# Row sums on VectorE beside the projections in place of modulation products in the attentions

## The chip, the cores and the metric

One Trainium2 chip, one core. The metric is the device time of one execution in microseconds (us), lower is better. The engines are TensorE (PE, its weight loads PEld), VectorE (DVE), ScalarE (ACT), GpSimd (POOL) and SyncE (SP), which here only issues DMAs.

## The reference, cut to what matters

The program is a two-layer image block with a context stream (512 image tokens, 256 context tokens, width 1024), followed by a two-layer second block, which the change leaves alone. All numbers are float32. In each layer of the first block, six vectors of 1024 values modulate the stream. They depend on a condition vector and on nothing that the layers compute:

```python
silu_c = jax.nn.silu(c)
silu_cc = jax.nn.silu(c_ctx)
for l in range(DEPTH):
    mod = silu_c @ w_ada[l] + b_ada[l]
    mod_c = silu_cc @ w_ada[l] + b_ada[l]
    sh1, sc1, gt1, sh2, sc2, gt2 = jnp.split(mod[:, None, :], 6, axis=-1)
    csh1, csc1, cgt1, csh2, csc2, cgt2 = jnp.split(mod_c, 6, axis=-1)
    h = modulate(rms_norm(x, norm1_g[l]), sh1, sc1)
    ...
    x = x + gt1 * merge_branches(ya, yb, ga, gb, w_proj_a[l], w_proj_b[l], w_out[l])
    h2 = modulate(rms_norm(x, norm2_g[l]), sh2, sc2)
    x = x + gt2 * swiglu(h2, w_ffn_gate[l], w_ffn_up[l], w_ffn_down[l])
```

`w_ada[l]` is 1024 by 6144, so a layer's modulation is a matrix of 24 MB used on two vectors. The context stream uses `csh1` to `cgt2` in layer 0, and in layer 1 only `csh1` and `csc1`.

## The kernel before

The kernel is written by hand, engine by engine, as a row of blocks (`nc.Block`), at whose ends all engines meet. Activations lie in SBUF with features on the partitions: `xL`, `xC` are the two streams, `arena` holds the projections (as `z`, in tiles of 128 features by 768 tokens), and the weights come as a stream of units of 128 by 1024 through a ring of four.

**Projections.** `project` runs a list of stages in one block. A stage (`Stage`) multiplies by its weight units, tile by tile. Every product is made of three (high times high, low times high, high times low half), so each unit is first split: ACT writes `w_high` (L450), DVE writes `w_low` (L453). There are two places for split units, so the unit for tile t+2 can only be split when PE has finished tile t. The results lie in two sets of PSUM banks that alternate. Per tile, an engine does in this order: the split of the unit two ahead (`split_ahead`), the eviction of this tile (`evict`), then what the parts in the stage's list `inner` put beside it. In the last tile before a norm (`norm_next`) the eviction comes first, then the split, then the `inner` parts. The block of layer 0 runs merge (8 tiles), out (8 tiles), gates and up (22 tiles with two units each), down, and the first projection of layer 1. A `Norm` stands ahead of the gates: PE sums squares (L560), ACT takes the root (L912), DVE refines it (`inverse_root`, L783 to L785), then DVE and ACT make the high and low halves (L932, L921, L947), for which PE waits. Meanwhile PE does products that nobody reads (L908).

**Attention.** `attention` goes over pairs of heads by 128 queries: 48 pairs in layer 0, of which the first 32 have 512 to 768 keys (long pairs below) and the last 16, with context queries, 256 keys (short pairs); 32 long ones in layer 1. At step i, PE does the scores of pair i (L1488), the turning of the probabilities of pair i-1 (L1504), and the values of pair i-2 (L1517). DVE takes maxima (L1544, L1547) and divides (L1564); ACT does the exponentials (L1591, L1598 for the sink), copies the turned probabilities (L1582) and the result (L1603). Scores of a long pair go to the banks of the pair before, so they wait for both its exponentials. Scores of short pairs alternate banks.

**Modulation.** The first third of layer 0's values comes ahead of everything (`FirstModulation`, unchanged). All others are made in the attentions by `ModulationBeside`: 32 units for the rest of layer 0 and 16 for the start of layer 1 in the first attention, 32 for the rest of layer 1 in the second. SP loads a unit in two halves (L731), PE multiplies it by the condition vectors in four products that stand in four column groups (L739), between the turning and the values of a step. At the end the sums go through ACT (L760), a product that picks rows (L748), ACT again (L763) and DVE (L684, L690). These products add to one PSUM bank that also holds the attention's results, so with modulation present ACT clears the result's part in every step (L1606), and PE's next values wait for that:

```python
if beside:
    pe.wait_ge(heads_out.sem, heads_out.at(j + 1))
elif j:
    pe.wait_ge(heads_copied.sem, heads_copied.at(j))
```

## Time and profile before

| | |
|---|---|
| median of 3 runs | 3494.99 us (3491.81 to 3496.72) |
| span of the profiled execution | 3496.1 us |
| PE busy | 3352.0 us, 96% |
| DVE, ACT, POOL busy | 47%, 35%, 12% |
| first projection of layer 0 (tiles 1 to 27) | 62 to 291 us |
| attention of layer 0, first product to first of the next block | 291.99 to 493.57 us |
| merge, out | 493.5 to 562.6, 562.6 to 630.5 us |
| norm, then gates | 630.5 to 642.6, 642.6 to 1010 us |
| attention of layer 1 | 1390.44 to 1551.09 us |

The profiled execution has only its span as a time of its own; it lies 1.1 us above the median of the runs. "Busy" on PE includes short products whose ends are modelled, so it overstates how full PE is.

### The profile page before, as it was taken

How to read it: one execution, taken by the hardware profiler on the slowest of the kernel's cores; microseconds unless marked ns; L12 is line 12 of the kernel's file. 1: busy time of each engine (PE TensorE's matmuls, PEld its weight loads, DVE VectorE, ACT ScalarE, POOL GpSimd, SP SyncE). 2: the span in 40 equal slices, each digit the busy share in tenths (PEclk: the TensorE clock that was granted, in tenths of full speed). 3: DMA queues.
4: the chain of work that ended last, by engine and by line, in shares of the span. 5: the costliest groups of instructions: out<-in, count | busy, mean ns of one | idle time of the engine just before them, and what ended most of it. 6: DMA issues, size and time to landing. Idle time of an engine off the chain costs nothing. (4 is left out here: it accounts for less than half of the span.)

```text
span 3496.1 us, 51241 instructions
## 1 busy us (share of the span) xinstructions
PE 3352.0 (96%) x21084; PEld 2656.6 (76%) x21084; DVE 1643.4 (47%) x2691; ACT 1223.3 (35%) x2135; POOL 423.3 (12%) x477
## 2 busy tenths in 40 slices
PE   6999999999999999999999999899999998999998
PEld 4887668788888787666787867657888777578886
DVE  4445754422132356665323347564443385744433
ACT  3215763321131222763223332353322332532322
POOL 0111110000000012112700133120000012210000
PEclk9999999999999999999999999999999999999999
DMA  5112331111212123322222322012222320022232
GB/s 210 61 60 99 109 122 66 50 66 61 67 61 73 55 79 101 129 70 97 90 91 91 105 89 67 20 37 92 96 95 98 102 85 9 31 91 95 92 99 82
DMA packets 89358, 287.61 MB, mean 82 GB/s; under 512 B 9904, under 2 KB 10288, under 8 KB 88752
## 3 DMA queue, kind: packets, MB, share of 16 engines
q1 hardware_dynamic: 89136, 284.41, 24.4%
q8 instruction: 168, 2.75, 0.3%
q14 instruction: 54, 0.44, 0.0%
HBM read 282.27 MB, written 2.10 MB: 81 GB/s over the span
## 5 line engine op out<-in xcount | busy, mean ns | idle before, releaser
L453 DVE TENSOR_TENSOR w_low<-ring,w_high 128x1024 fp32r<-128x1024 f32 x418 | 525.1, 1257 | 1523.2 <-ACT w_high L450 1522.6
L488 PE MATMUL ps<-arena_r,w_high 128*128 128x512 f32 x3568 | 1138.7, 384 | 10.1 <-PEq L1470 8.2
L450 ACT ACTIVATE w_high<-ring 128x1024 fp32r<-128x1024 f32 x418 | 442.8, 1060 | 1539.1 <-PE ps L488 1539.0
L488 PEld LDWEIGHTS ps<-arena_r,w_high 128*128 128x128 f32 x3568 | 646.1, 188 | 167.0 <-issue 15.6
L488 PE MATMUL ps<-low,w_high 128*128 128x512 f32 (+1 forms) x2448 | 765.0, 361 | 0.0
L488 PE MATMUL ps<-high,w_high 128*128 128x512 f32 x2368 | 735.8, 361 | 16.6 <-DVE low L947 8.6
L488 PE MATMUL ps<-high,w_low 128*128 128x512 f32 x2368 | 733.8, 360 | 0.0
L488 PE MATMUL ps<-arena_r,w_low 128*128 128x512 f32 (+1 forms) x1456 | 549.8, 390 | 0.0
L488 PEld LDWEIGHTS ps<-low,w_high 128*128 128x128 f32 x2448 | 410.8, 189 | 79.7 <-issue 1.1
L488 PEld LDWEIGHTS ps<-high,w_high 128*128 128x128 f32 x2368 | 394.2, 188 | 99.4 <-issue 12.2
L488 PEld LDWEIGHTS ps<-high,w_low 128*128 128x128 f32 x2368 | 393.7, 188 | 72.7
L488 PEld LDWEIGHTS ps<-arena_r,w_low 128*128 128x128 f32 x1456 | 267.0, 189 | 59.3
L549 POOL TENSOR_TENSOR tmp<-tmp 128x512 f32<-128x512 f32 (+1 forms) x42 | 60.9, 1451 | 1538.0 <-ACT tmp L539 1538.0
L1591 ACT ACTIVATE probs<-ps,stat 128x512 f32<-128x512 f32 (+3 forms) x224 | 153.0, 688 | 72.9 <-DVE stat L1549 34.8
L1488 PE MATMUL ps<-arena 64*128 64x256 f32 (+6 forms) x784 | 140.5, 431 | 19.0 <-ACT probs L1591 13.8
L1504 PE MATMUL ps<-const,probs 128*128 128x128 f32 x896 | 122.5, 279 | 15.8 <-DVE probs L1564 10.0
L1504 PEld LDWEIGHTS ps<-const,probs 128*128 128x128 f32 x896 | 98.2, 141 | 50.3 <-DVE probs L1564 39.4
L1582 ACT ACTIVATE probs<-ps 128x512 f32<-128x512 f32 (+3 forms) x224 | 120.8, 596 | 23.3 <-PE ps L1504 23.3
L488 PE MATMUL ps<-low,w_low 128*128 128x512 f32 x368 | 128.1, 376 | 0.0
L1488 PEld LDWEIGHTS ps<-arena 64*128 64x128 f32 (+1 forms) x784 | 79.2, 188 | 61.6 <-issue 32.5
L1517 PE MATMUL ps<-probs,arena 128*64 128x128 f32 x1792 | 123.0, 279 | 2.7 <-ACT hL L1603 1.3
L1517 PEld LDWEIGHTS ps<-probs,arena 128*64 128x64 f32 x1792 | 95.9, 137 | 38.4 <-issue 33.9
(359 smaller groups left out, 2866.0 us busy)
## 6 DMA issues: line engine op xcount, KB each, us to landing
ring<-in_weights SPq DMA_DIRECT2D x428, 512.0 KB, 3.4
hC<-in_ada SPq DMA_DIRECT2D x64, 256.0 KB, 3.0
high_f<-in_ada SPq DMA_DIRECT2D x40, 256.0 KB, 3.0
tmp<-in_ada SPq DMA_DIRECT2D x40, 256.0 KB, 3.5
arena<-in_ada SPq DMA_DIRECT2D x16, 512.0 KB, 15.6
arena<-in_ada SPq DMA_DIRECT2D x16, 256.0 KB, 4.0
xL<-in_x SPq DMA_DIRECT2D x1, 2048.0 KB, 10.0
out<-xL SPq DMA_DIRECT2D x4, 512.0 KB, 2.7
```

The costliest lines, as they stand in the source:

```text
L450: act.activation(w_high[:, slot, :], ring[:, place, :], ACT.Copy).then_inc(unit_high.sem, 1)
L453: dve.tensor_tensor(w_low[:, slot, :], ring[:, place, :], w_high[:, slot, :].bitcast(F32), ALU.subtract).then_inc(unit_free.sem, 1)
L488: mm = pe.matmul(bank(4 * (t % 2) + 2 * p + s, width), w, g.split[k][s][x], start=(n == 0 and m == 0), stop=(n == len(part) - 1 and m == 2))
L549: pool.tensor_tensor(tmp[:, 1, 0:total], tmp[:, 1, 0:total], tmp[:, 0, 0:total], ALU.add).then_inc(squares_sum.sem, 1)
L1488: mm = pe.matmul(ps[:, to:to + w], q, k, start=True, stop=True)
L1504: mm = pe.transpose(ps[:, to:to + P], probs[:, j % 3, e, m * P:m * P + P], con("ident"))
L1517: mm = pe.matmul(ps[e * HD:e * HD + HD, O_AT:O_AT + P], pair["values"][e][m], probs[:, j % 3, e, m * P:m * P + P], start=(m == 0 and not b ...
L1582: act.activation(probs[:, j % 3, e, 0:keys], ps[:, turned_at(j, e):turned_at(j, e) + keys], ACT.Copy).then_inc(turned_out.sem, 1)
L1591: act.activation(probs[:, i % 3, e, 0:keys], ps[:, scores_at(i, e):scores_at(i, e) + keys], ACT.Exp, bias=st[:, 2 + e:3 + e], scale=scale, ...
```

## The change

`ModulationBeside` is gone, and both calls of `attention` have no modulation beside them: 80 units of 512 KB are no longer loaded there, their products, the clearing of the result part (L1606) and the closing steps are gone. In their place the transposed weights come as 80 row tiles of 128 outputs by 1024 inputs (`ada_rows`), and DVE makes one value of each of 128 outputs with one `tensor_tensor_reduce` over 1024 inputs, with the condition vector repeated on all partitions (`cond_rows`, 128 by 2048, put through Silu on ACT). A row tile that both streams need takes two such steps, so there are 128 steps: 48 beside tiles 1 to 18 of the first projection, 24 beside the out stage (three in each of 8 tiles), 56 beside tiles 1 to 11 of the gates of layer 0. The second stream's step overwrites the loaded row tile, the first one's result goes to a spare place (PSUM banks 6 and 7 in the first projection). SP loads a row tile when the step that freed its place is done. The repeated condition is loaded and put through Silu three times: beside tile 0 of the first projection, of merge and of the gates.

```diff
+        class CondRows:
...
+            def scalar_parts(self, act, t):
+                if t == self.at:
+                    act.wait_ge(cond_in.sem, cond_in.at(16))
+                    act.activation(self.place, self.place, ACT.Silu).then_inc(cond_made.sem, 1)
...
+        class Rows:
...
+            def sync_parts(self, sync, t):
+                if t % self.units:
+                    return
+                for n, (source, _, _) in enumerate(self.jobs):
+                    if self.load_at[n] * self.units == t:
+                        if n == 0:
+                            sync.wait_ge(split_used.sem, stream["split"])
...
+                        if n >= len(self.slots):
+                            sync.wait_ge(row_used.sem, row_used.at(self.last[n - len(self.slots)] + 1))
+                        m = n % len(self.slots)
+                        sync.dma_start(self.slots[m], dram["ada_rows"][source]).then_inc(row_landed[m].sem, 16)
...
+            def scalar_parts(self, act, t):
+                if t == self.clear_at:
+                    act.wait_ge(row_used.sem, row_used.at(len(self.steps)))
+
+            def vector_parts(self, dve, t):
+                for m in self.by_tile.get(t, ()):
...
+                    if s == 0:
+                        dve.wait_ge(row_landed[place].sem, row_landed[place].at(16 * (n // len(self.slots) + 1)))
...
+                    ins = dve.tensor_tensor_reduce(out, self.slots[place], self.vectors[s], 1.0, 0.0, ALU.mult, ALU.add,
+                                                   mod[:, to, s:s + 1])
+                    ins.then_inc(row_used.sem, 1)
...
+        rows0 = Rows(row_jobs[:3 * KD],
+                     {1: 2, 2: 2, 3: 4, 4: 4, 5: 2, 6: 4, 7: 2, 8: 4, 9: 1, 10: 3, 11: 2, 12: 3, 13: 1, 14: 4, 15: 1, 16: 3, 17: 4, 18: 2},
...
-            if both:
-                rest = ModulationBeside(l, 8, 16, [1 + n for n in range(32)], places)
...
-                ahead = ModulationBeside(1, 0, 8, [36 + n * 12 // 16 for n in range(16)], again, rest)
-                attention(pairs1(l), HD ** -0.5, [rest, ahead])
-            else:
-                attention(pairs1(l), HD ** -0.5, [ModulationBeside(l, 8, 16, [1 + n * 28 // 32 for n in range(32)], places)])
+            attention(pairs1(l), HD ** -0.5)
...
+            rows1 = Rows(row_jobs[3 * KD:] + later[:4], {t: 3 for t in range(KD)}, cond1,
...
+            rows2 = Rows(mixed_jobs, {t: 5 if t < 11 else 6 for t in range(1, 12)}, cond2,
...
+            chain1 = [Stage([merge], sums, made=True, inner=[CondRows(cond1, 0)] if both else ()),
+                      Stage([out], Residual(16), inner=[rows1] if both else ())]
```

PE among the short pairs of the first attention. Before (L1517 values, L1488 scores, L1504 turning, L739 modulation; a row with x4 is four instructions):

```order
1570 L1517 MATMUL ps<-probs,arena 64x128 x4
1571 L1488 MATMUL ps<-arena 128x256 x2
1572 L1504 MATMUL ps<-const,probs 128x128 x4
1573 L739 MATMUL ps<-arena,cond 32x256 x4
1574 L1517 MATMUL ps<-probs,arena 64x128 x4
1575 L1488 MATMUL ps<-arena 128x256 x2
1576 L1504 MATMUL ps<-const,probs 128x128 x4
1577 L739 MATMUL ps<-high_f,cond 32x256 x4
1578 L739 MATMUL ps<-tmp,cond 32x256 x4
```

And at the same place with the change (L1562 values, L1533 scores, L1549 turning):

```order
1517 L1562 MATMUL ps<-probs,arena 64x128 x4
1518 L1533 MATMUL ps<-arena 128x256 x2
1519 L1549 MATMUL ps<-const,probs 128x128 x4
1520 L1562 MATMUL ps<-probs,arena 64x128 x4
1521 L1533 MATMUL ps<-arena 128x256 x2
```

The modulation products between turning and values are gone, one unit in some steps and two in others.

DVE at the end of the out stage of layer 0. Before (L1763 the residual of a tile, L453 the split, L783 to L785 the root of the norm, L932 its first products):

```order
588 L1763 SCALAR_TENSOR_TENSOR xL<-ps,mod,xL 128x512
589 L1763 SCALAR_TENSOR_TENSOR xC<-ps,mod,xC 128x256
590 L1763 SCALAR_TENSOR_TENSOR xL<-ps,mod,xL 128x512
591 L1763 SCALAR_TENSOR_TENSOR xC<-ps,mod,xC 128x256
592 L453 TENSOR_TENSOR w_low<-ring,w_high 128x1024
593 L783 SCALAR_TENSOR_TENSOR tmp<-ps,tmp 128x768
```

With the change (L1808 residual, L459 split, L802 a row sum with the reading of its result, L810 the bias, L828 the root):

```order
726 L1808 SCALAR_TENSOR_TENSOR xL<-ps,mod,xL 128x512
727 L1808 SCALAR_TENSOR_TENSOR xC<-ps,mod,xC 128x256
728 L459 TENSOR_TENSOR w_low<-ring,w_high 128x1024
729 L802 ISA arena,mod<-arena 128x1024
730 L802 ISA mod 128x1
731 L802 ISA arena,mod<-arena 128x1024
732 L802 ISA mod 128x1
733 L802 ISA arena,mod<-arena 128x1024
734 L802 ISA mod 128x1
735 L810 TENSOR_TENSOR mod<-mod,small 128x8 x2
736 L828 SCALAR_TENSOR_TENSOR tmp<-ps,tmp 128x768
```

Three row sums and the adding of the bias now stand between the split and the norm's root.

## Rows read from the trace of the kernel before

**Rows 1.** Stretches: length, busy us of each engine, PEclk, DMA share, GB/s

```profile
62.00:291.00 229.00, 228.97 (x1295) 197.58 (x1294) 96.81 (x114) 43.50 (x65) 25.68 (x20) 1.00 0.19 60
...
562.60:630.50 67.90, 67.55 (x387) 58.66 (x386) 22.05 (x31) 18.28 (x28) 11.07 (x6) 1.00 0.19 63
...
642.60:1010.00 367.40, 365.87 (x2087) 318.79 (x2088) 91.58 (x123) 75.23 (x110) 0.00 (x0) 1.00 0.19 61
...
2220.00:2240.00 20.00, 15.67 (x506) 14.10 (x503) 11.07 (x32) 2.94 (x6) 1.11 (x1) 1.00 0.02 4
```

**Rows 2.** Timeline of the first attention, two long pairs (start, us, engine, line, [idle before])

```profile
344.90 1.56 PE L1488 MATMUL ps<-arena 64*128 64x512 f32 x8 [0.23 <-ACT probs L1591]
...
347.88 0.64 PE L739 MATMUL ps<-hC,cond 128*32 128x256 f32 x8
348.45 1.53 PE L1517 MATMUL ps<-probs,arena 128*64 128x128 f32 x24
...
348.78 0.90 ACT L1591 ACTIVATE probs<-ps,stat 128x768 f32<-128x768 f32 x1
...
349.92 1.35 PE L1488 MATMUL ps<-arena 64*128 64x256 f32 x12
```

**Rows 3.** Timeline of the first attention, short pairs

```profile
464.56 0.70 PE L1488 MATMUL ps<-arena 64*128 64x256 f32 x4
...
467.36 0.70 PE L1488 MATMUL ps<-arena 64*128 64x256 f32 x4
...
468.00 0.46 ACT L1591 ACTIVATE probs<-ps,stat 128x256 f32<-128x256 f32 x1
...
468.90 0.47 ACT L1598 ACTIVATE stat<-small,stat 128x1 f32<-128x1 f32 x2
...
469.27 0.65 ACT L1582 ACTIVATE probs<-ps 128x256 f32<-128x256 f32 x2
...
469.74 0.70 PE L1488 MATMUL ps<-arena 64*128 64x256 f32 x4
...
470.16 0.28 ACT L1606 ACTIVATE ps<-const 128x128 f32<-128x128 f32 x1
...
470.38 0.46 ACT L1591 ACTIVATE probs<-ps,stat 128x256 f32<-128x256 f32 x1
```

**Rows 4.** Timeline of the second attention: a long pair without modulation, and the last values

```profile
1528.96 1.56 PE L1488 MATMUL ps<-arena 64*128 64x512 f32 x8
...
1533.97 1.13 PE L1488 MATMUL ps<-arena 64*128 64x256 f32 x8 [0.51 <-ACT probs L1591]
...
1547.83 1.53 PE L1517 MATMUL ps<-probs,arena 128*64 128x128 f32 x24 [1.15 <-ACT ps L1606]
```

**Rows 5.** Timeline of the end of the first attention

```profile
490.08 0.63 PE L748 MATMUL ps<-const,rows 128*128 128x32 f32 x4 [1.38 <-ACT ps L1606]
...
491.04 1.23 DVE L453 TENSOR_TENSOR w_low<-ring,w_high 128x1024 fp32r<-128x1024 f32 x1 [0.90 <-ACT w_high L450]
...
493.57 0.76 PE L488 MATMUL ps<-arena_r,w_high 128*128 128x512 f32 x1 [1.81 <-PEq L1470]
```

**Rows 6.** DVE groups of the whole span (busy us, mean ns of one)

```profile
L453 DVE TENSOR_TENSOR w_low<-ring,w_high 128x1024 fp32r<-128x1024 f32 x418 | 525.1, 1257 | 1523.2 <-ACT w_high L450 1522.6 <-PEq L787 0.3
...
L1544 DVE CUSTOM_DVE_ANT_0 ps<-ps,const 128x640 f32<-128x640 f32 x32 | 26.5, 827 | 2.5 <-PE ps L1488 2.5
...
L1544 DVE DVE_READ_ACCUMULATOR2_ANT stat<- 128x1 f32 x128 | 18.1, 141 | 0.0
...
L2208 DVE TENSOR_TENSOR high_f<-arena,other 128x1024 f32<-128x1024 f32 x2 | 4.6, 2309 | 0.0
```

**Rows 7.** Timeline of the norm ahead of the gates of layer 0

```profile
633.76 1.23 DVE L453 TENSOR_TENSOR w_low<-ring,w_high 128x1024 fp32r<-128x1024 f32 x1 [1.95 <-ACT w_high L450]
...
635.97 0.96 DVE L783 SCALAR_TENSOR_TENSOR tmp<-ps,tmp 128x768 f32<-128x768 f32 x1 [0.99 <-ACT tmp L912]
...
642.58 0.59 PE L488 MATMUL ps<-high,w_high 128*128 128x512 f32 x2 [1.30 <-DVE low L947]
```

More of the change, by code:

```diff
@@ new lines, in build, with __init__, tensor_parts @@
+        cond_in, cond_made, row_used = (count(n) for n in ("cond_in", "cond_made", "row_used"))
+        row_landed = [count(f"row_landed{n}") for n in range(4)]
+        class CondRows:
+            gpsimd = None
+            def __init__(self, place, at):
+                self.place, self.at = place, at
+            def sync_parts(self, sync, t):
+                if t == 0:
+                    sync.wait_ge(split_used.sem, stream["split"])
+                    if row_used.base:
+                        sync.wait_ge(row_used.sem, row_used.at(0))
+                    sync.dma_start(self.place, dram["cond_rows"]).then_inc(cond_in.sem, 16)
+            def tensor_parts(self, pe, t):
+                pass
+            def scalar_parts(self, act, t):
[3 more added lines that the diff above has]
+            def vector_parts(self, dve, t):
+                pass
+            def finish(self):
+                cond_in.base += 16
+                cond_made.base += 1
@@ L1296, in scalar, with input_projection @@
                                    bank(4 * (c % 2) + 1, C), ACT.Copy).then_inc(left_s.sem, 1)
-        def input_projection(l, normed):
+        def input_projection(l, normed, also=()):
             gemms = []
@@ L1866, in gemm, with mlp @@
             return g
-        def mlp(both, gate, normed, halves, after, beside=None, later=None):
+        def mlp(both, gate, normed, halves, after, beside=None, later=None, also=()):
             gates = gemm(KF, 2, 2, [[(0, k, k) for k in range(KD)], [(1, k, k) for k in range(KD)]], segments(both),
                          normed.split() if normed.late else split_h(both, hL, hC), not normed.late)
+            gates.z0 = 0
             down = gemm(KD, 4, 3, [[(k // 8, k % 8, k) for k in range(KF)]], segments(both), halves)
-            return [Stage([gates], Swiglu(halves, after, normed.late), normed, beside),
+            return [Stage([gates], Swiglu(halves, after, normed.late), normed, beside, also),
                     Stage([down], Residual(gate, later))]
@@ L1963, in build @@
             if both:
-                project(chain1 + mlp(both, 40, normed, halves, after) + [first_projection(1)])
+                project(chain1 + mlp(both, 5 * KD, normed, halves, after, also=[CondRows(cond2, 0), rows2]) + [first_projection(1)])
         Z2 = Z2_TILES * S
@@ L3007, in build @@
         into = LateNorm(lambda k: col("attn0", k), spare, lambda k: col("final1", k))
-        project(chain1 + mlp(False, 40, normed, halves, after, Trig(), into) + [second_projection(0, into, FirstFinal())])
+        project(chain1 + mlp(False, 6 * KD, normed, halves, after, Trig(), into) + [second_projection(0, into, FirstFinal())])
         for l in range(DEPTH):
```

137 lines of the change are left out of this document (70 added, 67 removed).

## Prediction

> **What bounds the kernel now.** I read the stretches of the stages first [rows 1]. In the first projection of layer 0, in out and in the gates, PE is busy for over 99% of the time, DVE for 42%, 32% and 25%: PE sets the end there, and DVE has room. Then the timelines of the attentions. Among the long pairs PE looks nearly full too, yet its scores wait 0.23 us for an exponential of ACT at 344.90 [rows 2]. The next scores start at 349.92; the exponential that they need began at 348.78 and took 0.90, and with the same 0.23 us they could not have started before 349.91. So the long pairs run in a ring: scores, maxima on DVE, two exponentials on ACT, scores. The modulation products (at 347.88; the values follow at 348.45, so 0.57 us of PE) lie in PE's slack. Among the short pairs it is different. There, scores start at 467.36 and 469.74 with no wait [rows 3]: 2.38 us for a pair, filled by four pieces of PE work. ACT has just as long a step where a sink is present, from 468.00 to 470.38, also without a wait.
>
> **What the removal gives: long pairs.** The second attention shows a step without modulation: scores at 1528.96 and 1533.97, 5.01 us, with a wait of 0.51 for ACT [rows 4]. The step from such a pair of 768 keys to the next takes 5.02 with modulation (344.90 to 349.92) [rows 2]. What PE no longer does turns into waiting. Some steps are bound by PE all the same (those whose exponentials are short, and those of the second attention that carry two units). Bounds for each attention: 0, since the ring remains, and 32 times 0.57, 18 us. I take 1.0 us for the first and 1.9 for the second, near the lower end, because both steps shown gain 0.01 or less.
>
> **Short pairs.** Without the 0.57 PE needs 1.81 us per pair. ACT loses the clearing, 0.22 us (470.16 to 470.38). That leaves 2.16 where there is a sink, and 1.79 where there is none, since the sink takes 0.37 (468.90 to 469.27) [rows 3]. They alternate, mean 1.97. So ACT becomes the limit, and DVE's division and maxima must keep up with it. The gain is 0.41 per step with one unit. With two units a step takes 2.80 (464.56 to 467.36), a gain of 0.83. Of the 12 steps that carry the 16 units, 8 have one and 4 two: 8 x 0.41 + 4 x 0.83 = 6.6. The picking product among the first short pairs gives 0.4. Bounds: 3 if DVE's chain adds 0.3 to each step, 9 if the steps before the 36th gain as much.
>
> **Ends.** At the end of the first attention PE waits 1.38 us for a clearing that stands behind the copy of the sums, does the picking product in 0.63, and only then the last values; the block after starts at 493.57. Without that, what remains is the second split, which ends at 492.27 [rows 5]. It moves up by the clearing and the copy ahead of it on ACT, some 0.7, and by the step's own gain. I take 1.4. At the end of the second attention the last values wait 1.15 us for the clearing [rows 4]. What ended just before it was the copy that they need as well, so less than that is gained: 0 to 1.15, I take 0.5.
>
> Together: 1.0 + 7.0 + 1.4 in the first attention, 1.9 + 0.5 in the second, 11.8 us.
>
> **What the row sums cost.** No row shows this operation with both sources in SBUF. The nearest are the same operation with one source in PSUM, 0.827 us for 640 elements plus 0.141 to read the result, and a product of two SBUF tiles of 1024 in 1.257 [rows 6]. Scaled, a step takes 1.26 + 0.14, so 1.4 us. Upper bound: 2.31 + 0.14, 2.45, from the row of 1024 elements that takes 2309 ns, when POOL works on SBUF at the same time. The whole is 128 x 1.4 = 179 us of DVE work, at no cost where it lies beside PE:
> First projection: DVE's 96.8 us over 28 tiles are 62 over 18; 48 steps add 67, and POOL's work there (25.7 in all, some 18 in these tiles) may stretch DVE by up to 15. That is 144 of 147 us. Out: 22 + 34 + some 8 for POOL's 11 = 64 of 68. Gates: 11 tiles of 16.7 are 184 us; DVE needs 46 + 78 = 124 [rows 1]. It fits everywhere, narrowly in the first projection. There DVE may fall some 6 us behind before PE notices: a split (1.26 us on DVE, behind about as much on ACT) must be ready one tile, 8.4 us, after PE has released its place. If the cover were gone, every further 0.1 us per step would cost 4.8 us. I take 0. SP's waits on row sums stand ahead of its weight loads, but those are four tiles early; ACT's one wait, at tile 18, has a tile of room. The three Silu of 128 x 2048, with table loads, fall on an ACT that is idle for three quarters or more of these stages.
>
> **The one place without cover.** After the last tile of out, DVE does its split at 633.76 to 634.99, waits 0.99 us for ACT, and starts the norm's root at 635.97; PE waits for what follows until 642.58 [rows 7]. Now three row sums (4.2) and the bias (0.2) stand in between: the root starts at 639.4, 3.4 us late. The residual of that tile also comes up to 0.5 late, since tile 6 needs some 9 us of DVE after its products (2.3 for the split on both engines, 1.1 for the residual, 4.2 for the sums, up to 1.4 beside POOL's sum), and a tile is 8.4. Everything behind is late by that. PE's filler products then run out, so it idles some 3 us more and may drop to 1.2 GHz for a few microseconds; 0.7 for that. Together 3.4 + 0.3 + 0.7 = 4.4, bounds 3 (a sum of 1.3, no drop) and 8 (a sum of 2.45).
>
> **Sum.** -11.8 + 4.4 = -7.4 us. Against the profiled execution that is 3496.1 to 3488.7 of span; against the median, 3495.0 to **3487.6**.
>
> **The rivals.** (1) **The row sums run at half rate and DVE becomes the bound**, the case on the other side. At 2.45 us, the first projection needs 62 + 118 + 15 = 195 us where 147 are there (+42 after the slack of 6), out 22 + 59 + 8 = 89 in 68 (+15), the norm 3 more, the gates 46 + 137 = 183 in 184. With the gain in the attentions: +60 + 4.4 - 11.8 = some +53, 3548. It decides from about 1.5 us per step; at 1.7 the loss in the first projection alone takes back the gain. For it: SBUF operands of DVE do take 2309 ns beside POOL [rows 6]; against it: 1257 for 418 of them otherwise. The Trainium skill (Vector Engine (DVE) Microarchitecture Reference, Points that are easy to get wrong) states such a rule: an accumulating two-tensor instruction with two SBUF sources that are not bf16 runs at half throughput, as no read port is left for the accumulator. No run here shows it yet; by that rule this rival's time would hold. I give it 0.12.
> (2) **The steps fit, but barely**: 1.5 to 1.7 us each, PE stalls of 3 to 10 us spread over the first projection: 3490 to 3498. 0.17.
> (3) **The clock drops inside the attentions**, because PE now has gaps: every stretch of it costs up to what PE then lacks. Against it: 2220 to 2240 with PE at 78% and the granted clock at 1.00 [rows 1], while the long pairs will have 85%. 0.08, 3490 to 3500.
> (4) **The attentions do not get shorter**: the short pairs keep their 2.38 through DVE's chain. Then only the ends remain, 2 us, and the norm costs 4.4: 3497. 0.06.
> (5) The gain is larger, the long pairs giving 3 us each and the norm little: 3482. 0.02. The forecast has 0.55.
>
> **How the numbers follow.** A measurement of this kernel tells 0.2%, 7 us, from no change; that bound is 3488.0. The forecast's own range is 3484 to 3491, and of its 0.55 I count 0.42 as faster, 0.13 as same, because the point lies almost on the bound. Rival 2 is same 0.12, slower 0.05; rival 3 same 0.05, slower 0.03; rival 4 same 0.04, slower 0.02; rival 1 slower 0.12; rival 5 faster 0.02. That makes 0.44 faster, 0.34 same, 0.22 slower. The range from 3482 to 3499 leaves out rival 1 and the tails of 2 and 3.
>
> **What the changed profile would show.** Right: row sums of 1.2 to 1.3 us with 0.14 behind, no PE wait for `w_low` from 62 to 291; short pairs at 1.97 on ACT, without waits; long pairs at the same period as before with larger waits for ACT; the norm ahead of the gates 3.5 to 4 us longer from the last product of out to the first of the gates. Wrong: row sums over 1.5 us, waits of PE for DVE's splits, a granted clock under 1.00 between the attention's first 20 us and its end, or a norm that is not later.

## The result, and the profile after

| | kernel before | changed kernel |
|---|---|---|
| median of 4 runs each, same chip | 3493.73 us (3491.81 to 3496.72) | 3477.23 us (3469.19 to 3481.14) |
| ratio to before | | 0.9943, 95% interval 0.9931 to 0.9955 |
| span of the profiled execution | 3496.1 us | 3479.2 us |

The change makes the kernel faster, by 16.5 us between the medians and 20 us by the ratio. The prediction said 7.4 us, so the direction is right, and the time lies below its whole range. I cut both traces at the first product of each stage, since the stages have different limits. The last two columns belong to two of the experiments, the last one to the fastest kernel of all, which comes at the end.

| us | before | changed | changed, weights at the old places | fastest kernel |
|---|---|---|---|---|
| to the first projection | 44.9 | 45.3 | 45.7 | 45.3 |
| first projection | 247.1 | 244.9 | 247.5 | 244.8 |
| first attention | 201.6 | 192.9 | 190.6 | 189.7 |
| merge to layer 1's projection | 896.9 | 892.3 | 898.1 | 886.5 |
| second attention | 160.6 | 160.5 | 157.9 | 157.0 |
| all that follows | 1945.0 | 1943.4 | 1944.0 | 1901.1 |

The rows show three surprises: the first projection got shorter although only work was added to it; so did the stages from merge on, which should have got longer by the norm; and the second attention gained nothing.

**What DVE does for the row sums.** This is `L802` of the changed kernel over the whole span (operation, count, duration in ns as minimum, median and maximum, first and last start), and then the stretch of [rows 1] again.

```profile
L802 DVE DVE_READ_ACCUMULATOR2_ANT mod<- x128: 75/83/144, 70.4 to 845.8; 128x1 f32 x128
L802 DVE CUSTOM_DVE_ANT_0 arena<-arena x104: 1212/1220/2875, 70.4 to 844.7; 128x1024 f32<-128x1024 f32 x104
L802 DVE CUSTOM_DVE_ANT_0 ps<-arena x24: 1216/1229/1234, 69.2 to 220.8; 128x1024 f32<-128x1024 f32 x24
```

```profile
62.00:291.00 229.00, 227.95 (x1305) 199.90 (x1306) 161.51 (x215) 49.54 (x70) 40.19 (x20) 1.00 0.32 111
```

A row sum takes 1.22 us, as long as a plain product of two such tiles [rows 6]; only where POOL works in SBUF at the same time does one take longer, 2.2 to 2.9, and not every one that does (the first beside a POOL instruction still takes 1.22). DVE is busy for 161.5 us where it was for 96.8 [rows 1], and PE stays at 228 of 229 us: the row sums cost PE nothing there that the profile shows.

**The norm ahead of the gates.** The timeline of the changed kernel, which answers to [rows 7]: start, length, engine, line, and in brackets the idle time before.

```profile
618.65 1.45 PE L566 MATMUL ps<-tmp,const 128*128 128x512 f32 x4
...
622.05 1.23 DVE L459 TENSOR_TENSOR w_low<-ring,w_high 128x1024 fp32r<-128x1024 f32 x1 [1.95 <-ACT w_high L456]
...
623.19 1.22 DVE L802 CUSTOM_DVE_ANT_0 arena<-arena 128x1024 f32<-128x1024 f32 x1
...
624.34 1.22 DVE L802 CUSTOM_DVE_ANT_0 arena<-arena 128x1024 f32<-128x1024 f32 x1
...
625.48 1.22 DVE L802 CUSTOM_DVE_ANT_0 arena<-arena 128x1024 f32<-128x1024 f32 x1
...
626.75 0.24 DVE L810 TENSOR_TENSOR mod<-mod,small 128x8 f32<-128x8 f32 x2
626.91 0.95 DVE L828 SCALAR_TENSOR_TENSOR tmp<-ps,tmp 128x768 f32<-128x768 f32 x1
...
633.51 0.77 PE L494 MATMUL ps<-high,w_high 128*128 128x512 f32 x1 [0.35 <-DVE low L992]
```

Three sums and the bias stand between the split and the root. The sums start 1.15 apart, not 1.4. From the split's start to the root's it is 4.86 us, where it was 2.21 [rows 7]: 2.65 later, and as much from the last product of out to the first of the gates (14.97 against 12.23, +2.74). TensorE's clock falls there as well, as the prediction had thought possible:

```profile
631.00:637.80 6.80, 6.37 (x15) 3.83 (x15) 6.67 (x14) 4.42 (x8) 0.00 (x0) 0.50 0.94 384
```

The columns are those of [rows 1], and the granted clock is 0.50. In the experiment with early row sums (below) it stays at 1.00 at the same place. Yet from the first product of the gates to the last of down both kernels take 551.3 us, so this fall costs nothing that shows.

**A short step and a long one.** The timeline of the first attention, which answers to [rows 3] and [rows 2].

```profile
461.92 0.70 PE L1533 MATMUL ps<-arena 64*128 64x256 f32 x4
...
463.83 0.70 PE L1533 MATMUL ps<-arena 64*128 64x256 f32 x4
...
465.85 0.70 PE L1533 MATMUL ps<-arena 64*128 64x256 f32 x4
```

```profile
344.62 1.56 PE L1533 MATMUL ps<-arena 64*128 64x512 f32 x8 [0.80 <-ACT probs L1636]
...
349.63 0.70 PE L1533 MATMUL ps<-arena 64*128 64x256 f32 x4 [0.50 <-ACT probs L1636]
```

Short steps now take 1.91 and 2.02, alternating: 1.97 on average, the predicted number, where it was 2.38. The steps themselves are not the predicted 2.16 and 1.79, and from 456 to 474 us PE, ACT and DVE are all nearly full (17.7, 17.3 and 16.9 of 18 us), so the profile doesn't show that ACT alone is the limit. The long step shown keeps its period, 5.01 against 5.02, and the wait for ACT grows from 0.23 to 0.80, which is the removed 0.57. That is the ring that the prediction described.

### The profile page after: what moved, and what is told of

Same layout as the page of the kernel before. It is cut to its first block and busy times, and to the rows that moved or that the text cites. A ratio compares the mean times of both kernels' runs of the same rounds, so it can differ in the third digit from the quotient of the medians.

```text
span 3479.2 us, 49806 instructions
## 1 busy us (share of the span) xinstructions
PE 3310.0 (95%) x20432; PEld 2653.7 (76%) x20432; DVE 1807.0 (52%) x2942; ACT 1210.4 (35%) x2054; POOL 445.8 (13%) x477
## 5 line engine op out<-in xcount | busy, mean ns | idle before, releaser
L459 DVE TENSOR_TENSOR w_low<-ring,w_high 128x1024 fp32r<-128x1024 f32 x418 | 526.8, 1260 | 1350.8 <-ACT w_high L456 1350.1
L494 PEld LDWEIGHTS ps<-arena_r,w_high 128*128 128x128 f32 x3568 | 646.8, 188 | 163.6 <-issue 16.9
L494 PE MATMUL ps<-high,w_high 128*128 128x512 f32 x2368 | 737.1, 362 | 15.1 <-DVE low L992 6.9
L1533 PE MATMUL ps<-arena 64*128 64x256 f32 (+6 forms) x784 | 143.3, 438 | 44.4 <-ACT probs L1636 38.4
L1533 PEld LDWEIGHTS ps<-arena 64*128 64x128 f32 (+1 forms) x784 | 83.1, 193 | 87.3 <-ACT probs L1636 54.0
L1549 PE MATMUL ps<-const,probs 128*128 128x128 f32 x896 | 126.5, 285 | 17.9 <-DVE probs L1609 8.9
L1549 PEld LDWEIGHTS ps<-const,probs 128*128 128x128 f32 x896 | 100.8, 144 | 54.3 <-DVE probs L1609 42.0
L802 DVE CUSTOM_DVE_ANT_0 arena<-arena 128x1024 f32<-128x1024 f32 x104 | 137.1, 1362 | 0.0
L1562 PE MATMUL ps<-probs,arena 128*64 128x128 f32 x1792 | 123.5, 280 | 2.8 <-ACT hL L1648 2.2
```

What stands on the lines that cost most here:

```text
L459: dve.tensor_tensor(w_low[:, slot, :], ring[:, place, :], w_high[:, slot, :].bitcast(F32), ALU.subtract).then_inc(unit_free.sem, 1)
L494: mm = pe.matmul(bank(4 * (t % 2) + 2 * p + s, width), w, g.split[k][s][x], start=(n == 0 and m == 0), stop=(n == len(part) - 1 and m == 2))
L802: ins = dve.tensor_tensor_reduce(out, self.slots[place], self.vectors[s], 1.0, 0.0, ALU.mult, ALU.add, mod[:, to, s:s + 1])
L1533: mm = pe.matmul(ps[:, to:to + w], q, k, start=True, stop=True)
L1549: mm = pe.transpose(ps[:, to:to + P], probs[:, j % 3, e, m * P:m * P + P], con("ident"))
L1562: mm = pe.matmul(ps[e * HD:e * HD + HD, O_AT:O_AT + P], pair["values"][e][m], probs[:, j % 3, e, m * P:m * P + P], start=(m == 0 and not b ...
```

## What shortened the stages that only got more work

I looked at the rhythm of the weight splits. ACT splits one unit for each one that PE finishes, so the distance of the splits is PE's time for a unit. These are the splits in the gates of layer 0, 31 of them (30 distances) in each kernel: before, changed, then two experiments (the kernel before with moved places, the changed kernel at the old places).

```profile
L450 ACT ACTIVATE w_high<-ring x31: 1060/1060/1060, 703.9 to 955.9; 128x1024 fp32r<-128x1024 f32 x31
```

```profile
L456 ACT ACTIVATE w_high<-ring x31: 1059/1059/1062, 694.3 to 943.9; 128x1024 fp32r<-128x1024 f32 x31
```

```profile
L450 ACT ACTIVATE w_high<-ring x31: 1058/1059/1059, 700.8 to 950.4; 128x1024 fp32r<-128x1024 f32 x31
```

```profile
L456 ACT ACTIVATE w_high<-ring x31: 1057/1060/1064, 695.5 to 947.5; 128x1024 fp32r<-128x1024 f32 x31
```

Before, 252.0 / 30 = 8.40 us a unit; changed, 249.6 / 30 = 8.32. The same 0.08 is missing in every stage that multiplies both streams, down and merge too, where the change adds no row sum; the stages of one stream keep 5.60. There are 116 such units, 9.3 us. The row sums couldn't do that. But the whole diff has one more line, which the excerpt under "The change" doesn't show: `MOD_COLS = 56` in place of 48. The table grows by 64 bytes in each partition, and everything allocated after it moves by 64 bytes: `tmp`, `work`, `rstd`, and `w_high` and `w_low`, which lie over `work`.

### The places alone, in the kernel before

```diff
-        mod, _ = at("mod", [P, 48, 2])
+        mod, _ = at("mod", [P, 56, 2])
```

> The kernel before with one edit: the table of modulation values gets 56 columns in place of 48, as the change gives it, and nothing uses the new ones. They take 64 bytes of each partition and so move all that is allocated behind them by 64 bytes: tmp, work, rstd and, lying over these, w_high and w_low. In the profile of the changed kernel every weight unit that is multiplied by both streams takes 8.32 us where it took 8.40, in all stages of layer 0, with row sums beside it or not; 116 such units (28 of the first projection, 8 of merge, 8 of out, 44 of the gates, 24 of down, 4 of the next projection) are 9.3 us. Theory A: the places of the weight halves in SBUF do this, and the change did it only by the way. Then this kernel takes 3493.7 - 9.3 = 3484.4 us, a ratio of 0.9973, with 8.32 us for a unit and unchanged attentions. Theory B: it comes with the change's own instructions (other DMAs, other work beside PE). Then 3493.7 and 8.40.

Measured: 3489.84 us against 3497.58 of the kernel before on that chip, ratio 0.9978 (0.9968 to 0.9989), 7.7 us; a unit takes 8.32 (third row above) and the attentions 201.6 and 161.2 as before. Theory A holds. A line that nobody would call part of the kernel's work is worth about as much (4 to 11 us) as the prediction's whole sum.

### The change without its side effect

```diff
-        mod, _ = at("mod", [P, MOD_COLS, 2])
+        mod, mod_at = at("mod", [P, MOD_COLS, 2])
...
-        decay_end, _ = at("decay_end", [P, 2, S // CHUNK])
+        decay_end, _ = at("decay_end", [P, 2, S // CHUNK], mod_at)
```

> The mirror of the run before it: the changed kernel, with decay_end (64 bytes of each partition, used in the second block only) laid over the modulation table, so that tmp, work, rstd, w_high and w_low stand where the kernel before had them. Theory A (the places): a unit of both streams takes 8.40 us again, and the whole 3477.2 + 9.3 = 3486.5 us. Theory B: 8.32 us and 3477.2. By A this run is also the change itself without its side effect, and by the two profiles it should stand some 7.6 us below the kernel before.

Measured: 3485.96 us, ratio 0.9962 (0.9949 to 0.9976); 8.40 us a unit (fourth row above). So the change itself is worth 13 us (8 to 18) and the places 8 (4 to 11). The profile of this run is also the clean one for the change: first attention 10.9 us shorter, second 2.7, norm 2.65 longer, and 12.1 in all. The 1.2 that these three leave over come from merge and out, 1.75 shorter, and from the rest, 0.6 longer; the profiles don't show a cause for either.

### The attentions alone

```diff
-                attention(pairs1(l), HD ** -0.5, [rest, ahead])
+                attention(pairs1(l), HD ** -0.5)
...
-                attention(pairs1(l), HD ** -0.5, [ModulationBeside(l, 8, 16, [1 + n * 28 // 32 for n in range(32)], places)])
+                attention(pairs1(l), HD ** -0.5)
...
+                dve.memset(mod[:, 16:48, :], 0.25)
+                dve.memset(gain[:, 1, :, :], 1.0)
```

> The kernel before with both attentions called without modulation beside them. The computation is changed: all modulation values but those of the first norm are constants, set once. All places in SBUF are those of the kernel before. It shows what the attentions alone give, and against the changed kernel at the same places what the row sums cost. By the two profiles the first attention gives 10.6 us and the second 2.9 apart from their first two steps, which took 4.7 us more in the profiled run of the changed kernel, at a granted clock of 0.5 for 13.7 us each; so 3480.2 us where the clock stays up there and 3484.9 where it falls. If the row sums cost only the norm ahead of the gates (2.75 us by the profiles), this is 2.7 us below the changed kernel at the old places; if they also stretch PE's tiles or the waits elsewhere, it is further below.

Measured: 3483.44 us, ratio 0.9963 (0.9949 to 0.9977). The medians of this run and of the changed kernel at the old places, on the same chip, lie 2.5 us apart, and the profiles show 2.65 in the norm. Between the ratios no difference can be told. The 128 row sums, 179 us of DVE work in the prediction, show no cost but these 2.6 us, though by the intervals of the two ratios several microseconds more or less could hide. The first attention takes 190.9 us here and 190.6 there.

### The row sums' one visible cost

```diff
-            rows1 = Rows(row_jobs[3 * KD:] + later[:4], {t: 3 for t in range(KD)}, cond1,
+            rows1 = Rows(row_jobs[3 * KD:] + later[:4], {t: 3 + (1 < t < 5) for t in range(KD - 1)}, cond1,
...
-                         [(KD - 1, 0, 5 * KD, KD, 5 * KD, 2, None)], False)
+                         [(KD - 2, 0, 5 * KD, KD, 5 * KD, 2, None)], False)
```

> The changed kernel with the 24 row sums of the out stage beside tiles 0 to 6 (three each, four in three of them) in place of 0 to 7, so that none stands between the last split and the norm's root. Theory: the three sums and the bias are all that makes the norm later; the root starts 2.7 us earlier, 5.5 us behind the last product of out as in the kernel before (5.51 there, 8.26 with the change), and the time is 2.7 us lower. Rival: what is late is ACT's table load or the residual, then 0 to 1.

One run: 3472.47 us, 4.8 below the median of the changed kernel, which one run can't tell from the expected 2.7. The profile decides; the timeline of the norm:

```profile
619.10 1.45 PE L566 MATMUL ps<-tmp,const 128*128 128x512 f32 x4
...
622.78 1.23 DVE L459 TENSOR_TENSOR w_low<-ring,w_high 128x1024 fp32r<-128x1024 f32 x1 [1.95 <-ACT w_high L456]
...
624.99 0.96 DVE L828 SCALAR_TENSOR_TENSOR tmp<-ps,tmp 128x768 f32<-128x768 f32 x1 [0.99 <-ACT tmp L957]
...
631.61 0.59 PE L494 MATMUL ps<-high,w_high 128*128 128x512 f32 x2 [1.31 <-DVE low L992]
```

The root starts 2.21 us after the split, as before the change, with the same wait of 0.99 for ACT. From out's last product (618.98) to the gates it is 12.63, 2.3 less than in the changed kernel. The 0.4 that is left comes ahead of the split: the last sum beside tile 6 runs against POOL for 2.87 us, and the residual follows it. The mechanism holds.

### Where the cover ends

```diff
+                    if self.clear_at:
+                        if m:
+                            dve.wait_ge(row_used.sem, row_used.at(m))
+                        chain_v.link(dve, dve.tensor_tensor_reduce(self.spare, self.slots[place], self.vectors[s], 1.0, 0.0,
+                                                                   ALU.mult, ALU.add, mod[:, to, s:s + 1]))
                     ins = dve.tensor_tensor_reduce(out, self.slots[place], self.vectors[s], 1.0, 0.0, ALU.mult, ALU.add,
```

> The changed kernel with each of the 48 row sums of the first projection made twice (the first result is not used), which loads DVE as the prediction's first rival would have. DVE is busy for 124 of the 149 us from 62 to 211; 48 more of 1.36 and a wait of some 0.1 each make 194. If the cover ends where the prediction says (some 6 us of lag, then every us of DVE is one of the whole), the first projection takes 38 us more, 3515 in all. If DVE's busy time overstates what it needs, less, down to 20.

One run: 3525.16 us, and the first projection takes 293.4 us, 48.4 more, where 38 were expected. First the changed kernel in the stretch that carries 45 of its 48 sums, then this one.

```profile
62.00:211.00 149.00, 149.00 (x850) 130.47 (x850) 123.94 (x166) 35.83 (x49) 30.55 (x14) 1.00 0.38 134
```

```profile
62.00:260.00 198.00, 173.38 (x909) 147.21 (x908) 188.21 (x256) 38.14 (x52) 31.39 (x14) 0.93 0.30 103
```

DVE is busy for 188 of 198 us and sets the pace, and PE has gaps. Its granted clock falls to 0.93 on average, 28 us at 1.2 GHz, which can account for some of the 10 us by which the expectation was short; how they divide between the clock and DVE's remaining idle time isn't settled by this run. By this run the prediction's first rival, half rate, would have cost what it said or more: only its premise was false.

## What the distance between weights and data does

A pair in this section is a product of 512 columns with one of 256 behind it, by the same weights, as the two streams need it; a unit of both streams is 24 such pairs, a unit of one stream 24 products of 512 columns.

```python
for k in range(8):
    for m in range(3):
        for s, width in enumerate(widths):
            pe.matmul(ps[:, s * 512:s * 512 + width], w[:, k % 4 * P:k % 4 * P + P], x[:, s * 512:s * 512 + width], ...)
```

> A kernel that computes nothing of the reference: PE alone multiplies, as the projections do (128 by 128 weights, fp32r, 24 products of 512 columns each followed by one of 256, then the same with 512 columns alone), 16 sets of weights whose place in a partition is 0, 32, 64 ... 480 bytes beyond a multiple of 512, and one set with the moving data at 0, 64 ... 448 bytes beyond a multiple of 512. Theory A in its simplest form: a pair of products takes 0.350 us at 32 bytes and 0.347 at 96, and other places give other times; perhaps also the products of 512 columns alone, 0.233 us in all later stages, depend on the place. If all 16 take the same, the place matters only beside the other engines' traffic, or it is not the place of the weights.

These are stretches of PE alone, each one set of 72 pairs (first six) or 72 products of 512 columns (last two); the columns are the stretch, its length, PE busy with its count of records, the granted clock, DMA share and GB/s. The weights lie 0, 32, 96, 160, 224, 256 and then 160, 256 bytes past a multiple of 512; the data lies at one.

```profile
97.09:122.05 24.96, 24.96 (x146) 1.00 0.00 1
122.05:147.47 25.42, 25.42 (x146) 1.00 0.01 1
172.90:197.87 24.97, 24.97 (x146) 1.00 0.00 1
223.15:248.35 25.20, 25.20 (x146) 1.00 0.00 1
273.48:298.44 24.96, 24.96 (x147) 1.00 0.00 1
298.44:323.88 25.44, 25.44 (x147) 1.00 0.00 1
784.98:801.79 16.81, 16.81 (x74) 1.00 0.00 1
...
835.07:851.40 16.33, 16.33 (x73) 1.00 0.00 0
```

Divided by 72 and times 2.4 GHz, with all 16 places and the eight places of the data, the table is (cycles for a pair, for one product of 512 columns):

```
distance, weights minus data, modulo 256:   0    32    64    96   128   160   192   224
pair of 512 and 256 columns               848*  847   848   832   843   840   837   832
512 columns alone                         545   560   560   562   558   560   550   560
* 848 at 256 bytes, 832 at 0 in this run
```

Moving the data has the effect of moving the weights the other way: weights at 32 and data at 64, 128, 192, 256 give 832, 841, 832 and 848, within 1 of the distances 224, 160, 96 and 32. In the kernel all moving data (`low`, `high`, `arena`) starts 128 bytes past a multiple of 256; `w_high` stood at 209440 before, a distance of 160, and stands at 209504 with the change, 224. The table gives 840 and 832 cycles for a pair, and a unit of 24 pairs then takes 8.40 and 8.32 us: just what both profiles show. It also shows what the stages of one stream could gain: 560 cycles for a product of 512 columns, where 545 can be had at a distance of 0.

> The changed kernel with tmp and all behind it moved by another 32 bytes, so that w_high and w_low begin at 209536, a whole number of 512 bytes from the moving data (57472, 82048 and 106624 bytes). What the run of PE alone showed depends only on the distance from the moving data to the weights, modulo 256 bytes: a pair of 512 and 256 columns took 840 cycles of 2.4 GHz at a distance of 160 (as in the kernel before), 832 at 224 (as in the changed kernel) and 832 at 0; a product of 512 columns alone took 560 at 160 and at 224, but 545 at 0. Theory A: the same holds in the kernel. The 302 units of one stream, 24 products each, then take 5.45 us in place of 5.60, 45 us in all, and the 116 of both streams stay at 8.32: some 3432 us, a ratio of 0.982 to the kernel before. Theory B: the 545 is not to be had beside the other engines' traffic, or a pair goes to 848 as the table shows for an even multiple of 256: then 3477 to 3496.

```diff
+        place["end"] += 32
         tmp, _ = at("tmp", [P, 2, T])
```

Measured: 3450.95 us, ratio 0.9869 (0.9852 to 0.9885). The splits in the gates, and in a stretch of one stream that was 5.60 us a unit in all kernels so far:

```profile
L457 ACT ACTIVATE w_high<-ring x31: 1060/1060/1062, 699.7 to 954.1; 128x1024 fp32r<-128x1024 f32 x31
...
L457 ACT ACTIVATE w_high<-ring x32: 1060/1060/1061, 1707.6 to 1876.2; 128x1024 fp32r<-128x1024 f32 x32
```

168.6 / 31 = 5.44 us: 544 cycles a product, as theory A said. But 254.4 / 30 = 8.48, 848 cycles a pair, as theory B said. I had read the table's one 832 at distance 0 as the rule. Nineteen more microseconds went that way, and the result is 3451 where I expected 3432. A second run of PE alone was to tell which it is.

> PE alone again, nothing of the reference computed. In places_alone a pair of products took 832 cycles at a distance of 0 and 848 at 256 bytes, and aligned, at a distance that is a multiple of 512, took 848. So the distance modulo 256 doesn't tell all for a pair. Here the weights go through 32 places 256 bytes apart with the moving data in two regions, then the second moving piece, the PSUM banks, steps of 8 bytes in the distance, and narrower products. If the place of the second moving piece or its distance to the first decides, its own row of sets shows it; if it is a larger stride (512 to 8192), the 32 places do; if it is the banks, theirs. A product alone should take 544 or 545 at every multiple of 256.

All 32 places, with the data in either region, gave 848.0 cycles a pair at distance 0 modulo 256, as did other distances of the second piece (847 to 848) and other PSUM banks. A product alone took 544.0 in seven sets, and 550 in the two sets that came right behind pairs (these two are also the only ones at the first of the places). The first two rows are 768 pairs each, the third 168 products.

```profile
47.06:318.42 271.36, 271.36 (x1539) 1.00 0.00 1
318.42:589.78 271.36, 271.36 (x1539) 1.00 0.00 1
595.28:633.36 38.08, 38.08 (x170) 1.00 0.00 0
```

The same set at distance 0 took 832 in one run and 848 in the other; what separates them stays open. Finer steps matter too: at 8, 16 and 24 bytes a pair takes 838, 834 and 832.

## A kernel with both rates, and the second attention

A distance of 224 gives pairs 832 in every run, products alone want 0, and these are 32 bytes apart. So the first 112 units use a view of the weight halves that lies 32 bytes lower:

```diff
+        def halves_of(unit):
+            return (w_high_near, w_low_near) if unit < BOTH_UNITS else (w_high, w_low)
...
+                    first = stream["split"] + v == BOTH_UNITS
+                    act.wait_ge(split_used.sem, v + (stream["split"] + (0 if first else 1 - SPLIT)))
```

> The changed kernel with the weight halves at two places and the early row sums. In the run aligned (w_high at 209536) a unit of both streams took 8.48 us, 848 cycles for a pair of products, and a unit of one stream 5.44 (544 cycles for a product); 32 bytes lower, at 209504 as in the changed kernel, it was 8.32 and 5.60. Here the first 112 units (both streams) use the lower place and all others the upper one; ACT's first split at the upper place waits for the unit before, which falls on the norm ahead of layer 1's projection. The row sums of out stand beside tiles 0 to 6. Theory A (the place alone sets the rate, unit by unit): 112 units at 8.32, 4 at 8.48, 302 at 5.44, so 48 us less than the changed kernel from the later stages, 0.6 more from the four, 2.3 less from the norm: 3477.2 - 49.7 = 3427.5, between 3424 and 3434. Against aligned (3451.0) this is 112 x 0.16 + 2.3 = 20.2 us. Theory B: something else in aligned made its gain, and the sum isn't reached.

Measured: 3434.63 us, just above the expected range, on a chip where the kernel before takes 3498.95. The ratio is 0.9817 (0.9803 to 0.9830), 64 us where 66 were expected, and both rates hold (below: the near place in the gates, 8.32; the other in a stretch of one stream, 163.2 / 30 = 5.44).

```profile
L465 ACT ACTIVATE w_high_near<-ring x31: 1059/1059/1062, 688.6 to 938.2; 128x1024 fp32r<-128x1024 f32 x31
...
L465 ACT ACTIVATE w_high<-ring x31: 1060/1060/1060, 1707.6 to 1870.8; 128x1024 fp32r<-128x1024 f32 x31
```

The same edit of the places, with the table of 56 columns, in the kernel before:

> The kernel before, modulation in the attentions as it was, with the two places of the weight halves alone. By theory A: 116 units 9.3 us faster less 4 x 0.16, 302 units 48 us faster: 3494 to 3497 less 57, so 3438 to 3440, a ratio of 0.984. The difference between this run and the changed kernel at two places is what the change itself is worth, some 8 us before the early row sums, 10 with them. Were the change and the places to hang together, the two would differ by less or more than that.

Measured: 3449.32 us, ratio 0.9860 (0.9845 to 0.9876). The places are worth 49 us (43 to 54) without the change at all, where the expectation's ratio meant 56; the profile shows 50. The expectation missed: it gave 0.16 us to each of the 302 units of one stream, but in the kernel before only some 224 of the distances between their splits are 5.60 us, which may be the reason. The kernel above lies another 15 us lower, where 10 were expected, with some 7 us of uncertainty. Some of this is what the profiles differ by without a known cause: all that follows the second attention took 1937.8 to 1945.0 us in the seven profiles whose code and places give it the same rates.

**Why the second attention gained nothing.** PE at its start, in the changed kernel:

```profile
1375.41 1.15 PE L1533 MATMUL ps<-arena 64*128 64x128 f32 x12 [1.05 <-PEq L1289]
1379.47 2.93 PE L1533 MATMUL ps<-arena 64*128 64x512 f32 x8 [2.91 <-ACT probs L1636]
...
1385.81 2.50 PE L1533 MATMUL ps<-arena 64*128 64x256 f32 x12 [1.51 <-ACT probs L1636]
1388.24 2.82 PE L1549 MATMUL ps<-const,probs 128*128 128x128 f32 x12
```

The twelve turning products take 2.82 us where they take 1.53 at full clock. The clock of these stretches (again the columns of [rows 1]):

```profile
1375.41:1378.50 3.09, 1.15 (x12) 0.95 (x12) 1.83 (x6) 2.02 (x3) 0.00 (x0) 1.00 0.01 3
1378.50:1392.10 13.60, 11.12 (x50) 8.37 (x52) 6.95 (x19) 6.52 (x17) 0.00 (x0) 0.50 0.01 1
```

PE falls to 1.2 GHz within its idle time of 2.91 us and stays there for 13.6 us, with the gap of 1.51 us in them. It is so at the start of the first attention too (granted clock 0.60 from 290.27 to 307.29). With modulation, products stood in the last of these gaps; the clock fell there as well, but for less long (granted clock 0.77 to 0.89 up to the scores of pair 3). From the first scores to those of pair 3 it took 14.5 to 15.1 us in all six starts of the three profiles with modulation. In the fourteen starts of the seven profiles without it, it took 16.0 to 17.2 in nine and 14.2 to 15.0 in five. So the change seems to make a slow start likelier, which gives back up to 2.7 us in each attention; the profiled run of the changed kernel has two of them.

> The changed kernel with nine products of 128 by 512 that nobody reads in PE's idle time of the first two steps of each attention (six behind the scores of pair 0, three behind the turning of pair 0). The first two steps took 17.0 and 17.2 us in the profile of the changed kernel and 14.7 and 14.6 in that of the changed kernel at the old places; in three profiles with modulation 14.5 to 15.0. Theory: PE's idle time there brings the clock down at random, and the fillers hold it: 14.5 to 15.0 always, the median 2 us lower. Rival: what comes before (the end of the block, PE waiting for ACT and DVE) decides, and nothing changes or the fillers delay the scores of pair 1 by up to 1 us.

```diff
                         if 0 <= i - 1 < n:
                             turn(i - 1)
+                        if i < 2:
+                            for _ in range((6, 3)[i]):
+                                pe.matmul(bank(7), con("mean_all"), const[:, 0:BANK], start=True, stop=True)
```

Measured: 3489.21 us, ratio 0.9979 (0.9970 to 0.9989), 12 us slower than the changed kernel. The clock did hold (granted clock 1.00 at both starts), but a product of this kind takes 0.90 us. Six of them fill 5.42 us where PE idled for 2.91, so pair 3 comes after 16.2 us at full clock. And `attention` is called twice more in the second block, where I had not meant to add them: "all that follows" takes 1951.8 us, 8.4 more, more than the 8.0 us between the two profiles. The theory was right about the clock, the rival about the delay, and the fillers were too long.

The second try, on top of the kernel with two places and early row sums:

```diff
+                        if i < 2 and not more:
+                            for _ in range((3, 1)[i]):
+                                pe.matmul(bank(7), con("mean_all"), const[:, 0:BANK], start=True, stop=True)
```

> The kernel with two places and early row sums, and in the two attentions of the first block four products that nobody reads: three behind the scores of pair 0, one behind the turning of pair 0. In the run filled such a product took 0.90 us, six of them 5.42 where PE idles for 2.91 only, so the scores of pair 1 came 2.4 us late; but no clock of 0.5 was recorded at the start of either attention. Three take 2.7 and fit into the 2.91, one takes 0.9 and fits into 1.50. Theory: the clock stays at 1.0 there and the first steps take the same time in every run, which takes 0 to 2.6 us from each attention, 2 to 3 from the median: 3431 to 3433, ratio 0.981. Rival: PE's idle time that is left is enough for the clock to fall all the same, and nothing changes (3434.6).

Measured: 3426.40 us (3424.23 to 3433.30), ratio 0.9797 (0.9784 to 0.9810). From its trace:

```profile
290.14 1.15 PE L1542 MATMUL ps<-arena 64*128 64x128 f32 x12 [1.05 <-PEq L1298]
291.21 2.84 PE L1583 MATMUL ps<-const 128*128 128x512 f32 x6
294.20 1.56 PE L1542 MATMUL ps<-arena 64*128 64x512 f32 x8
...
296.62 1.02 PE L1583 MATMUL ps<-const 128*128 128x512 f32 x2
299.17 1.35 PE L1542 MATMUL ps<-arena 64*128 64x256 f32 x12 [1.52 <-ACT probs L1648]
300.45 1.53 PE L1558 MATMUL ps<-const,probs 128*128 128x128 f32 x12
...
303.81 1.56 PE L1542 MATMUL ps<-arena 64*128 64x512 f32 x8 [0.80 <-ACT probs L1648]
```

The fillers at 291.21 and 296.62 (three and one; the profile shows each as two instructions) delay nothing that shows, and the twelve turning products take 1.53. Pair 3 comes after 13.7 us, less than in any other profile. The ratios of this kernel and of the one without fillers overlap at their ends, so the 7 us between them (8 between the medians) are likely but not certain; the 14.6 and 16.0 us that the starts took there account for 3.3. This is the fastest version: 71 us below the kernel before.

## Why the prediction was wrong, point by point

**The forecast's sum leaves out a term.** The step that failed is the line "-11.8 + 4.4 = -7.4", which keeps every tile of the projections at the length that it had; "a tile, 8.4 us" was used as given. Measured, it is 8.32: a term of -9.3 us by the profiles (-7.7 by the run with the places alone) that no part of the prediction speaks of, though the whole diff had its line. With it the sum would have been 3478.3, and the median was 3477.2. That is partly luck, since the terms below are off in both directions. Of the change without its side effect the profile shows -12.1, not -7.4.

**Long pairs: right.** The ring sets the period (5.01 after, 5.02 before), and what PE no longer does becomes waiting. Between pair 3 and pair 32 the first attention gained 1.6 (1.0 predicted), between pair 3 and pair 31 the second 2.5 (1.9). Both came from the steps that I had named as bound by PE: 4.43 became 4.05, four times in the first.

**Short pairs: right in the gain, not in the steps.** 1.97 a step on average, as worked out; 7.4 us against 7.0. The working was steps of 2.16 and 1.79 on ACT, and the steps are 1.91 and 2.02, with PE, ACT and DVE all nearly full. That the average agrees is partly luck.

**Ends: right.** 1.6 against 1.4, and 0.35 against 0.5.

**Row sums under cover: right, and with more room than thought.** "A step takes 1.4": it is 1.22 to 1.23 without POOL, from start to start 1.15, and 1.31 on average over the 45 sums from 62 to 211 us. DVE is busy for 124 of 149 us there, not 144 of 147 (the prediction also divided a stretch of 27 tiles by 28; with 27 it would have been 147 of 153). PE never waits for it.

**The norm: right mechanism, oversized.** "Together 3.4 + 0.3 + 0.7 = 4.4" measured 2.7. The root is 2.65 late, since three sums take 3.4 and not 4.2, and 0.1 is left for the residual. The clock did fall, to 0.50 for 6.8 us, and costs nothing that shows, where the prediction had 0.7.

**Rivals.** (1) Half rate: false. The Trainium skill (Vector Engine (DVE) Microarchitecture Reference, Points that are easy to get wrong) has an accumulating two-tensor instruction with two SBUF sources that are not bf16 at half throughput. For this kernel's row sum the trace disagrees with the rule as the prediction applied it: 1.22 us for 1024 fp32 elements, the time of a plain product. The page states it for one instruction format (`S2S2D2_STT`), and the profile, which calls the row sum `CUSTOM_DVE_ANT_0`, doesn't show whether it has that format. The 0.12 rested on the page and on the row of 2309 ns beside POOL. What it would have cost was shown by doubling the sums. (2) Barely fit: false, PE waits for no split from 62 to 291 us. (3) The clock: true in a form I had not written down. Not inside the attentions, where the granted clock is 1.00 (310 to 480 us), but in their first 17 us, where PE has three gaps. Up to 2.7 us each. (4) Attentions not shorter: false, 10.9 and 2.7 us with the weights at the old places. (5) Larger gain: true in sign, but its reason, the long pairs and a cheap norm, explains 3 of the 12.5 us that were missing by the ratio.

**The range** was made of bounds on the terms that I had, so a term that was missing lay outside it.

## What to carry to other kernels

Read a diff for what it does to addresses too. An edit that enlarges an early buffer moves all later ones, and a comparison of two versions then measures both. Look at one number that should not change (here the time of a weight unit in a stage that the edit doesn't touch), and repeat the comparison with the old addresses. And where PE is full for most of a kernel, sweep the distance between its weights and its data in one small run: 1.4% of this kernel lay there, more than the change was worth. In the gaps at a stage's start, a few unread products that fitted the gap kept the clock up here, and too many cost time.

## What the runs showed of the hardware

- PE's time for an fp32r product of 128 by 128 weights, with a weight load for each, depends on the distance in the partition between the weights and the moving data, modulo 256 bytes: 544 to 562 cycles of 2.4 GHz for 512 columns, and 832 to 848 for a pair of 512 and 256. The best distance is not the same for the two (0 and 224). PE alone shows it, so it isn't other engines' traffic. The Trainium skill (TensorE: Matmul & The Clock Gate, Step-by-step: what each phase is for) says that PE reads weights and moving data through two independent ports, and that loading the next weights takes no bandwidth from the running product. The runs don't show how the two meet, only that the place of one against the other costs up to 3%.
- At distance 0 a pair took 832 cycles in one run of PE alone and 848 in another and in the kernel. Why is open.
- An fp32 `tensor_tensor_reduce` with both sources in SBUF takes 1.22 us for 1024 elements, no longer than a plain product of two such tiles (1.26), and up to 2.9 beside POOL.
